# Expert visits: gated rows kept in a DRAM scratch and fetched back by token, in place of a running sum in PSUM

## What is computed

```python
# h: the normed tokens, 256 x 1024
logits = h @ o_router                    # 8 experts
top2, gates = two largest, softmax over the two
for e in range(8):
    y_e = (silu(h @ moe_gate[e]) * (h @ moe_up[e])) @ moe_down[e]   # width 3584
x = x + sum over a token's two experts of gate * y_e
```

## Time and profile before

| | |
|---|---|
| time, median of 3 runs | 2558.63 us (2558.61 to 2559.03) |
| the profiled execution | 2560.24 us, span 2558.4 us |
| PE busy | 2494.5 us, 98% of the span |
| DVE busy | 1929.0 us, 75% |
| ACT busy | 1499.3 us, 59% |
| POOL busy | 129.4 us, 5% |
| DMA, mean | 242 GB/s, 619.83 MB |
| granted TensorE clock, mean | 0.997 of full speed |

### The profile page before, as it was taken

How to read it: one execution, slowest core, us unless ns; L and a number is a source line. 1 busy time by engine, 2 the same in 40 slices (tenths; PEclk the granted TensorE clock), 3 DMA queues, 4 the chain that set the end, 5 groups by cost and what they waited for, 6 DMA issues and landing times.

```text
span 2558.4 us, 41983 instructions
## 1 busy us (share of the span) xinstructions
PE 2494.5 (98%) x15961; PEld 2113.2 (83%) x15961; DVE 1929.0 (75%) x2674; ACT 1499.3 (59%) x2177; POOL 129.4 (5%) x108
## 2 busy tenths in 40 slices
PE   8899999989999999999999999999999999999998
PEld 7676999857888888888888888857999999876998
DVE  7856555758999999999999997777656655688655
ACT  5613435447888888878887886393444443257432
POOL 0100000006301010100000000000000000010000
PEclk9999999999999999999999999999999999999999
DMA  6646543687999999999999995202554552231551
GB/s 262 247 191 255 190 184 116 235 327 288 379 354 378 359 371 361 368 365 369 367 366 370 363 360 220 115 2 115 206 183 167 197 191 104 99 132 75 222 188 50
DMA packets 90973, 619.83 MB, mean 242 GB/s; under 512 B 10209, under 2 KB 10465, under 8 KB 40801
## 3 DMA queue, kind: packets, MB, share of 16 engines
q1 hardware_dynamic: 88992, 609.17, 62.1%
q0 software_dynamic: 1280, 4.72, 0.5%
q10 hardware_dynamic: 576, 4.19, 0.5%
HBM read 615.95 MB, written 2.10 MB: 242 GB/s over the span
## 4 chain that ended last, share of the span: by engine, by line
PE 85%; DVE 9%; ACT 3%; DMA 2%; issue 1%; DVEq 0%; SPq 0%; ACTq 0%
PE psum L2032 8%; PE psum L2034 8%; PE psum L2033 8%; PE psum L436 7%; PE psum L438 7%; PE psum L437 7%; PE psum L2069 4%; PE psum L2067 4%; PE psum L2068 4%; PE psum L451 3%; PE psum L452 3%; PE psum L453 3%; DMA ring<-stream_dram 2%; PE psum L1515 1%; PE psum L2041 1%; PE psum L2591 1%
## 5 line engine op out<-in xcount | busy, mean ns | idle before, releaser
L2402 DVE TENSOR_TENSOR r_high<-ring,r_high 128x1024 fp32r<-128x1024 f32 x670 | 799.0, 1231 | 56.1 <-ACT r_high L2285 42.8
L2285 ACT ACTIVATE r_high<-ring 128x1024 fp32r<-128x1024 f32 x672 | 703.3, 1062 | 76.7 <-PE psum L2034 53.1
L436 PE MATMUL psum<-r_low,r_high 128*128 128x256 f32 x1408 | 399.5, 284 | 2.1 <-DVE r_high L526 1.1
L438 PE MATMUL psum<-r_low,r_high 128*128 128x256 f32 x1408 | 398.4, 283 | 0.0
L2032 PE MATMUL psum<-r_high 128*128 128x512 f32 x896 | 359.5, 401 | 2.0 <-DVE r_high L2393 2.0
L2034 PE MATMUL psum<-r_high 128*128 128x512 f32 x896 | 350.4, 391 | 0.0
L2033 PE MATMUL psum<-r_high 128*128 128x512 f32 x896 | 350.2, 391 | 0.0
L526 DVE TENSOR_TENSOR r_high<-ring,r_high 128x1024 fp32r<-128x1024 f32 x263 | 306.0, 1218 | 9.5 <-ACT r_high L485 9.2
L437 PE MATMUL psum<-r_high 128*128 128x256 f32 x1056 | 298.8, 283 | 0.0
L499 ACT ACTIVATE arena<-psum 128x256 f32<-128x256 f32 x88 | 33.8, 384 | 434.7 <-PE psum L438 431.9
L436 PEld LDWEIGHTS psum<-r_low,r_high 128*128 128x128 f32 x1408 | 269.9, 192 | 7.8 <-DVE r_high L3174 1.5
(11 more groups left out here) (645 smaller groups left out, 4522.1 us busy)
## 6 DMA issues: line engine op xcount, KB each, us to landing
ring<-stream_dram SPq DMA_DIRECT2D x160, 1536.0 KB, 6.6
ring<-stream_dram SPq DMA_DIRECT2D x224, 1024.0 KB, 6.9
ring<-stream_dram SPq DMA_DIRECT2D x224, 512.0 KB, 6.3
arena<-bias_dram ACTq DMA_DIRECT2D x2, 1024.0 KB, 7.7
pack<-pack_dram SPq DMA_DIRECT2D x1, 1664.0 KB, 16.9
const<-const_dram SPq DMA_DIRECT2D x1, 1060.0 KB, 13.3
x<-x_dram SPq DMA_DIRECT2D x1, 1024.0 KB, 5.0
xc<-ctx_dram ACTq DMA_DIRECT2D x1, 1024.0 KB, 5.5
```

The source lines that it names most:

```text
L436: pe.matmul(dst, hi, f["x_hi"][:, k, :], start=(k == 0 and part == 0), stop=False)
L438: ins = pe.matmul(dst, lo, f["x_hi"][:, k, :], start=False, stop=(k == KD - 1 and part == 1))
L2285: act.activation(dst, src, ACT.Copy).then_inc(sem("moe_w_hi"), 1)
L2402: ins = eng.tensor_tensor(lo, src, hi.bitcast(f32), SUB)
```

## The change

The loop visits add nothing on PE any more. ACT evicts the down sum times the gate once, in plain float32 (`oute`), and POOL writes these 128 rows to a DRAM scratch `y_rows`, 128 rows per visit. DVE's part `oute_lo` falls away in them, as do the transposes of `pick` and their copies; the gate of the next visit is taken as a third column of the product that gives the indices in pair 6. `first_sum` is gone; idle matmuls stand where parts of it stood. The last visit still adds through PE (with start=True), and POOL adds the others: from the tables it works out, for each token, which rows of `y_rows` hold its two gated results (`moe_back_pool`, ahead of its loop), with one row of zeros for "none". In the last visit it gathers these rows, two DMAs of 128 rows and two adds of 128 x 1024 into x, and then the same again. ACT waits for these adds before its last eviction, and DVE adds the PSUM sum to x in place of a copy. Rows of `y_rows` that may be read without being written are filled early, at the first feed-forward layer, by three POOL DMAs. `y` rows of a visit are 512 KB.

```diff
         def first_weights_pool(pool):
             split_dve(pool, swiglu, ffn_at("e_ffn", 0, 0), 0, 1, 2)
+            pool.wait_ge(sem("pack_in"), 32)
+            for v in range(N_EXP - 1, MAX_VISITS - 1):
+                pool.dma_start(y_rows[v * P:(v + 1) * P, :], const[:, 0:D]).then_inc(sem("moe_rows_in"), 16)
...
-            if p in (1, 2):
+            if p in (1, 2) and not more:
                 ins = pe.transpose(spare[0], pick[:, p - 1, :].bitcast(f32), ident)
-            if p == 1:
+            if p == INDEX_AT and more:
                 for j in range(NT):
-                    ins = pe.matmul(spare[1][:, 0:1], pick[:, j, :].bitcast(f32), gate_t[:, j:j + 1],
-                                    start=(j == 0), stop=(j == NT - 1))
-            if p == INDEX_AT and index:
-                for j in range(NT):
-                    ins = pe.matmul(spare[0][:, 0:2], pick[:, j, :].bitcast(f32), token_of[:, j, :],
+                    ins = pe.matmul(spare[0][:, 0:3], pick[:, j, :].bitcast(f32), token_of[:, j, :],
                                     start=(j == 0), stop=(j == NT - 1))
...
-            def first_sum(j, hf):
-                pe.matmul(psum[:, 2 * j + hf, :], ident, x_tm[:, j, hf * 512:(hf + 1) * 512], start=True, stop=False)
-
-            for hf in range(2):
-                first_sum(0, hf)
+            idle_pe(pe, 1)
             route_turn_pe(pe, 1)
-            first_sum(1, 0)
...
-            first_sum(1, 1)
-            idle_pe(pe, 1, 5, 256)
+            idle_pe(pe, 1, 5)
...
             pe.wait_ge(sem("moe_tables"), 1)
+            for j in range(NT):
+                pe.matmul(psum[:, 0, 0:1], pick[:, j, :].bitcast(f32), token_of[:, j, 2:3],
+                          start=(j == 0), stop=(j == NT - 1))
...
                 pe.wait_ge(sem("moe_out_act"), 2 * v + 2)
+                if more:
+                    return
                 for j in range(NT):
                     for hf in range(2):
-                        pe.matmul(psum[:, 2 * j + hf, :], giveT[:, j, :], oute_hi[:, hf, :], start=False, stop=False)
+                        pe.matmul(psum[:, 2 * j + hf, :], giveT[:, j, :], oute_hi[:, hf, :], start=True, stop=False)
...
                 else:
                     l0_piece_act(act, 1)
-                    moe_out_act(act, v)
+                    act.wait_ge(sem("ctx_xn"), 9)
+                    moe_out_act(act, v, False)
...
             moe_more_visits_pool(pool)
             moe_more_values_pool(pool)
+            moe_back_pool(pool)
             n_more = moe_more(pool)
-            pool.wait_ge(sem("moe_rows_in"), 16)
+            pool.wait_ge(sem("moe_rows_in"), BACK0)
             with pool.Fori(0, n_more) as v:
...
-                pool.wait_ge(sem("moe_rows_in"), v * 16 + 32)
+                pool.wait_ge(sem("moe_rows_in"), v * 32 + (BACK0 + 16))
                 pool.sem_inc(sem("pool_step"), 1)
                 pool.tensor_scalar(slot_x, slot_x, slot_rstd, None, MUL).then_inc(sem("pool_out"), 1)
+                pool.wait_ge(sem("moe_out_act"), 2 * v + 2)
+                pool.sem_inc(sem("pool_step"), 1)
+                pool.dma_start(y_rows[bass.ds(v * P, P), :], oute).then_inc(sem("moe_rows_in"), 16)
+            pool.wait_ge(sem("moe_rows_in"), n_more * 32 + BACK0)
+            pool.sem_inc(sem("pool_step"), 1)
+            for n in range(2):
+                pool.wait_ge(sem("ctx_xn"), (2, 7)[n])
+                if n == 0:
+                    moe_back_index_pool(pool)
+                for j in range(NT):
+                    pool.indirect_dma_start(back_x[j], None, y_rows,
+                                            bass.IndirectOffsetOnAxis(back_i[:, 2 * n + j:2 * n + j + 1], 0))\
+                        .then_inc(sem("moe_rows_in"), 16)
+                pool.wait_ge(sem("moe_rows_in"), n_more * 32 + (BACK0 + 32 * n + 32))
+                pool.sem_inc(sem("pool_step"), 1)
+                for j in range(NT):
+                    pool.tensor_tensor(x_tm[:, j, :], x_tm[:, j, :], back_x[j], ADD).then_inc(sem("ctx_xn"), 1)
+
+        def moe_back_pool(pool):
+            S(pool.memset(back_zero[0:1, :], 0.0))
+            for hf in range(2):
+                pool.dma_start(y_rows[BACK_NONE:BACK_NONE + 1, hf * 512:(hf + 1) * 512], back_zero[0:1, :])
...
+            S(pool.tensor_scalar(by_visit(back_at), visits, float(P), -float(BACK_NONE), MUL, ADD))
+            S(pool.tensor_tensor(back_at, back_at, vpos, ADD))
+            S(pool.tensor_scalar(back_ok, vpos, 0.0, None, ALU.is_ge))
+            S(pool.tensor_scalar(back_tmp, vpos, float(CAP), None, ALU.is_lt))
+            S(pool.tensor_tensor(back_ok, back_ok, back_tmp, MUL))
+            S(pool.tensor_scalar(by_visit(back_tmp), visits, plan_f[:, 12:13], None, ALU.is_lt))
+            S(pool.tensor_tensor(back_ok, back_ok, back_tmp, MUL))
+            S(pool.tensor_tensor(back_ok, back_ok, vsel, MUL))
+            S(pool.tensor_tensor(back_at, back_at, back_ok, MUL))
+            S(pool.tensor_tensor(back_tmp[:, 0:12], back_at[:, 0:12], back_at[:, 12:24], ADD))
+            S(pool.tensor_tensor(back_tmp[:, 0:6], back_tmp[:, 0:6], back_tmp[:, 6:12], ADD))
+            S(pool.tensor_tensor(back_tmp[:, 0:2], back_tmp[:, 0:2], back_tmp[:, 2:4], ADD))
+            step(pool, pool.tensor_tensor(back_tmp[:, 0:2], back_tmp[:, 0:2], back_tmp[:, 4:6], ADD), "pool_out")
...
-            step(pool, pool.tensor_scalar(vpos[:, 2 * N_EXP:2 * MAX_VISITS], vpos[:, 2 * N_EXP:2 * MAX_VISITS], -float(CAP),
-                                          None, ADD), "pool_out")
+            S(pool.tensor_scalar(vpos[:, 2 * N_EXP:2 * MAX_VISITS], vpos[:, 2 * N_EXP:2 * MAX_VISITS], -float(CAP), None, ADD))
...
             for j in range(NT):
+                if j == 0:
+                    dve.wait_ge(sem("ctx_xn"), 9)
                 dve.wait_ge(sem("moe_sum"), j + 1)
-                step(dve, dve.tensor_copy(x_tm[:, j, :], psum[:, 2 * j:2 * j + 2, :].rearrange("p b n -> p (b n)")),
-                     "moe_x")
+                step(dve, dve.tensor_tensor(x_tm[:, j, :], x_tm[:, j, :],
+                                            psum[:, 2 * j:2 * j + 2, :].rearrange("p b n -> p (b n)"), ADD), "moe_x")
```

More of the change, by code:

```diff
@@ L1946, in program @@
         INDEX_AT, GATHER_AT = 6, 8
+        BACK0 = 96
         x_rows = nc.dram_tensor("x_rows", (NT * P, D), f32).ap()
+        BACK_NONE = (MAX_VISITS - 1) * P
+        y_rows = nc.dram_tensor("y_rows", (BACK_NONE + 1, D), f32).ap()
+        back_i = ar(9912, 2 * NT).bitcast(i32)
+        back_f = ar(9916, 2 * NT)
+        back_at, back_ok, back_tmp = [ar(9920 + 2 * NV * i, 2 * NV) for i in range(3)]
+        back_zero = ar(9008, 512)
+        back_x = [ar(6144, D), oute]
         slot_x = ar(0, D)
-        token_of = tables[:, 296:300].rearrange("p (j n) -> p j n", j=NT)
+        token_of = tables[:, 296:302].rearrange("p (j n) -> p j n", j=NT)
         slot_rstd, slot_index = ar(9908, 1), ar(9910, 1).bitcast(i32)
@@ L2036, in moe_gate_up_pe, with moe_transpose_pe @@
                     ins.then_inc(sem("moe_gu"), 1)
-        def moe_transpose_pe(pe, at, p, chunks=(), ctx_parts=(), index=False):
+        def moe_transpose_pe(pe, at, p, chunks=(), ctx_parts=(), more=True):
             pe.wait_ge(sem("moe_h32"), at[2] + 1)
@@ L2249, in visit @@
                 pe.wait_ge(sem("moe_out_act"), 2 * v + 2)
+                if more:
+                    return
                 for j in range(NT):
                     for hf in range(2):
[L2252 to L2253 removed]
+                        pe.matmul(psum[:, 2 * j + hf, :], giveT[:, j, :], oute_hi[:, hf, :], start=True, stop=False)
+                pe.wait_ge(sem("moe_out_dve"), 1)
                 for j in range(NT):
                     for hf in range(2):
[L2256 to L2259 removed]
+                        ins = pe.matmul(psum[:, 2 * j + hf, :], giveT[:, j, :], oute_lo[hf], start=False, stop=True)
+                    ins.then_inc(sem("moe_sum"), 1)
             with pe.Fori(0, n_more) as v:
@@ L2296, in moe_stage_act @@
             if out is not None:
-                moe_out_act(act, out)
+                moe_out_act(act, out, True)
             if between:
@@ L2310, in moe_stage_act, with moe_out_act @@
                 moe_split_act(act, nxt, p + 1, 5, 6)
-        def moe_out_act(act, v):
+        def moe_out_act(act, v, more):
             act.wait_ge(sem("moe_dn"), v * NB_EXP + (NB_EXP + AHEAD))
             for hf in range(2):
-                act.activation(oute_hi[:, hf, :], psum[:, 4 + hf, :], ACT.Copy, scale=gate_s)\
+                dst = oute[:, hf * 512:(hf + 1) * 512] if more else oute_hi[:, hf, :]
+                act.activation(dst, psum[:, 4 + hf, :], ACT.Copy, scale=gate_s)\
                    .then_inc(sem("moe_out_act"), 1)
@@ L2406, in moe_split_lo, with moe_stage_dve @@
                     ins.then_inc(e_used[r + q // 4], 1)
-        def moe_stage_dve(dve, at, nxt, p, out=None, xe_next=None, index=False):
```

(13 more changed lines are left out.)

34 lines of the change are left out of this document (22 added, 12 removed).

## The result

| | median, us | runs | against before, 95% interval |
|---|---|---|---|
| kernel before | 2559.19 (2556.8 to 2563.11) | 22 | |
| changed kernel | 2564.05 (2559.16 to 2569.76) | 22 | 1.0018 [1.0012, 1.0024] |

The changed kernel is 4.9 us slower (0.19%, just inside the 5.1 us that the prediction calls no change), where 0.1 to 0.7 us slower was forecast. The interval, 3.1 to 6.1 us, leaves out both none and the forecast: a small loss is real. It also scatters more: 10.6 us between its lowest and highest run, against 6.3. The profiled execution took 2569.76 us, the longest of the 22.

The account below looks back on a forecast made before the run. PE, busy 98%, sets the pace, with DVE and DMA queues close behind. Costs 10.7 + 1.6 + 4.0 + 1.5 = 17.8 us against 17.1 gain: +0.7, 2559.3 us; own range 2554 to 2564, with rivals 2549 to 2570.

Parts of the forecast that it names:

- gain in PE's work, less the writes and gathers: Loop and last visits: sums, transposes and gate product leaving PE save 17.1 us; writes cost 1.5, gathers' chain nothing.
- work ahead of the first gather, with the clock: Visit 0: POOL's added work stops PE for 10.7 us, and the slower clock behind it costs 1.6.
- POOL's adds of the last visit, against DVE's: Last visit: POOL's adds hold up DVE and so PE, 2.0 us a round, 4.0 us for two rounds.
- The first stall: Ahead of pair 8 of visit 0, PE waits 10.7 us for POOL's first fetched and scaled rows.
- The chain of the step: Ahead of the first gather: 14.8 us added path, less 1.6 slack and 2.5 from faster scaling, stops PE 10.7 us.
- the return of the scaling and the clock: Visit 0: scaling gives back 2.5 us while PE waits; half clock afterwards costs 1.6 us.
- Rival (a): Ahead of the first gather, POOL's added steps are cheap: 3.3 us stall, clock stays, 2550.3 us; chance 0.16.
- The writes: Loop visits: each writes 0.52 MB more into the weight stream, a quarter microsecond in six visits, 1.5 us.
- rival (b): Early in each visit the DMA queue becomes the bound: 8.4 us in place of 1.5, 2566.2 us; chance 0.20.
- rival (c): Last visit's adds stop PE 3.4 us a round, each dropping the clock: 10.0 us, total 2565.3 us; chance 0.12.
- The lock: Last visit: each two-input POOL add holds DVE up for 2.2 us, two in a row for 4.4.
- what can DVE spare: Last visit: DVE idles 0.55 and 0.52 us in a pair and its hidden product leads PE by 1.0 us.

Follow-up runs that it names:

- e9: e7 with the zero row's memset and two writes moved directly behind POOL's write of the tokens' rows; 2544.05 us.
- e6: Changed kernel with POOL's tables behind its loop, DVE doing the last visit's adds, and its four gathers issued one at a time; 2549.44 us.
- e4: Changed kernel with the four adds of the last visit done by DVE, POOL only gathering; 2558.32 us.
- e2: Changed kernel without POOL's four adds in the last visit, gathers and index steps kept; 2556.29 us.
- b1: Kernel before without the eight summing matmuls in the seven loop visits, nothing else changed; 2547.46 us.
- e3: e2 with the four gathers of the last visit left out too, index steps kept; 2555.45 us.
- e1: Changed kernel with POOL's 13 table steps moved behind its loop and DVE's reduction into the last visit; 2557.89 us.
- e7: e6 with the zero row's memset and two writes moved ahead of POOL's split share; 2546.85 us.
- e10: e9 with each loop visit writing its gated rows a second time, to another scratch; 2543.34 us.
- a_repeat: The changed kernel run once more, unchanged, beside the kernel before; 2563.71 us.

## Why the prediction was right or wrong

The forecast of no change held, but only at its upper edge: 2564.05 us, where its own range ended at 2564. By medians the runs give each term (the stretch that was changed, and between which runs). That the last column adds up to the net says nothing, since each row starts at the run at which another ends:

| term | predicted | measured | from |
|---|---|---|---|
| gain in PE's work, less the writes and gathers | 17.1 - 1.5 = 15.6 | 15.1 | before and e9 |
| work ahead of the first gather, with the clock (and 0.6 of e6) | 12.3 | 14.3 | e4 and e9 |
| POOL's adds of the last visit, against DVE's | 4.0 | 5.7 (7.8 against no adds, e2) | changed and e4 |
| net | +0.7 | +4.9 | |

**The gain was right.** 1.80 us a visit for the sum (b1), and 119.87 less 119.2 is 0.67 for the transposes and the gate product, 0.66 in the prediction. By the middle columns e9 is 7.8 + 8.5 = 16.3 us shorter than before; with the 1.0 us of the gathers added back (e3 against e2) that is 17.3, for the predicted 17.1. That the first row of the table comes so near is partly luck: 1.5 us was charged for writes that cost next to nothing, and nothing for gathers that cost about 1.0.

**The first stall was right in kind and place, and 2 us too small** (the table's 14.3 less 12.3). The chain of the step holds with the measured pieces: 15.5 us of added path (659.99 to 675.47; predicted 14.8), less 1.6 of slack, less 1.7 that the faster scaling gave back (4.60 to 2.86; I took 2.5), is 12.2; PE stood 12.1. (Smaller differences cancel: the gather landed 0.55 us sooner, and against POOL's first mark the added path began 0.2 us later and PE came 0.3 us sooner.) What was mis-sized is the return of the scaling and the clock: half clock lasted 5.2 us, 2.4 to 2.6 lost, where I took 1.6 from a stop of 2 us. The stretch behind that short stop was no measure for the one behind a stop of 12. The price of a small POOL step was 1.04 us (13 in 13.5 us) for the 0.91 taken; memset and issues took 2.0 us for the 3.0 taken, and the two nearly cancel. Rival (a) fell. But e2's execution, 9.7 us for the same 13 steps, shows that this mean is a mixture of two values, and that rival (a) is partly a matter of how the steps fall. I had written that short and long steps exist, and should have carried the scatter that follows into the result's own.

**What I did not see at all** is that the zero row's two writes were on this path by themselves. I priced their issue (2.1 us), and took the wait in front of the loop, which also counts their landing, at nothing, naming no cover. The tables were the cover. e1 laid it bare (3.6 us), and e7 and e9 removed it.

**The writes cost next to nothing.** Nearly all visits with them take 119.1 to 119.6 us; two single ones took 119.84 (e1) and 120.11 (e3). I took 1.5 us, and gave rival (b) 0.20. ACT's waits for weights grew to microseconds a visit, 15.4 us in all, which I had listed as a sign of (b); as such it misled. They fall where ACT is ahead. A wait of a producer is not a price until it has used up its lead; I read that lead as 1.5 us, from one pair; it is more, for in e10, with 19 waits of ACT of up to 2.5 us, PE stops for 0.9 us in all. The Trainium skill ("DMA: Bandwidth & Descriptors", Where 436 GB/s comes from) puts the HBM side at about 358 GB/s for a core, half of what it gives for a stack. That is no bound for this kernel, which runs on one core: e10's visit moved 382 GB/s for 119 us.

**The last visit was mis-sized too**, and rival (c) came true in part. The lock was right to a tenth: 4.3 us for two adds, 4.4 predicted, as the Trainium skill's rule of whole-instruction exclusion also has it ("SBUF — State Buffer", Who interferes with whom). So was the case of adds that straddle two pairs, 1.3 predicted and 1.43 measured, and nearly that of two adds in one pair, 2.3 and 2.60.

One failed step is "what can DVE spare". I gave DVE both idle gaps and its lead of 1.0 us. In the first round it had neither. Undisturbed it ends its hidden product 3.83 us after it begins its three products (1479.15 to 1482.98). From 1488.85 that is 1492.7, and PE had come at 1491.88: 0.8 us late without any lock, and 0.8 + 4.3 = 5.1, the measured 5.15. In a_repeat 1505.62 + 3.83 is 1509.5 against PE's 1508.94: 0.6 + 4.4 = 5.0, the measured 4.93. Both times ACT had just waited 1.7 to 2.0 us for weights. That the gathers were the reason is my guess and not shown, for ACT waited as long where no gather was under way.

The other failed step is that I put no loss of clock into this term, though I put one behind the first stall; rival (c) had 1.6 us for each stop. The stops of 5.15 and 2.60 us brought half clock for 4.7 and 3.5 us, 4 us lost; the one of 1.43 us in a_repeat brought none. 8.0 + 4 = 12 us is most of the 12.6 by which the column of the last visit is longer than e3's. In the repeat that difference is 10.2, while the medians say 5.7 to 8.6. Why the medians are lower than both executions I can't show; the profiled executions were not the middle ones (e2's took 2548.11 us with a median of 2556.29, e3's 2557.56 with 2555.45).

**The signs** came as listed: the PE wait near 677 ended by POOL's scaling, the loop visits at 119.2, POOL's steps to 675.5, DVE's long products beside the adds. Of the PE waits of the last visit, forecast at 1 to 3 us, one was in the range (2.60) and one out of it (5.15).

## What to carry to other kernels

Before handing a two-input SBUF operation to GpSimd to spare VectorE, compare what GpSimd takes from VectorE while it runs with what VectorE would need itself: here 2.2 us against 1.22, so the hand-over lost even though GpSimd was idle. A new use of an idle engine should be laid in its idle time, not at the end of its current work: the same 13 table steps and one zero row cost 14.3 us ahead of the first gather and nothing that a run here could tell behind the loop and behind an earlier write. And when a wait counts several transfers, name for each what hides its landing.

## What the runs showed of the hardware

- A POOL step on 24 columns or fewer beside a busy DVE mostly takes one of two values, 0.2 to 0.3 us or 1.0 to 1.4, rarely 0.6 to 0.7 or 2.2 to 2.3. Identical code gave 9.7 us and 13.5 us for 13 such steps in two executions, and 6.2 and 12.1 us of PE wait.
- POOL's two-input add of 128 x 1024 adds 2.0 to 2.2 us to DVE's work, also where two adds straddle two groups of DVE. Its one-input scaling of the same size took 2.86 to 3.17 us in the eight executions in which PE stood waiting for it, and 2.85 to 4.9 us in later visits beside a busy DVE.
- With the writes the transfers of this one core ran at 376 to 383 GB/s for whole visits, and at 1475 to 1480 us of e2 at 425.
- After PE stops of 12.1, 5.15, 2.60 and, in the kernel before, 2.0 us the granted clock was at half (1.2 of 2.4 GHz) for 5.2, 4.7, 3.5 and 3.5 us. After stops of 1.43 us (a_repeat) and 0.87 us (e2) it stayed full.
